# First norm's squares by ScalarE alone; splits, banks and fills around the last RWKV pairs; compression groups with ScalarE's copy of transposed probabilities

## The reference

```python
h = rms_norm(x, norm_mix_pre[l])
z = h @ w_in[l]
z_rwkv, z_nsa, z_gate = jnp.split(z, [RWKV_COLS, RWKV_COLS + NSA_COLS], axis=-1)
o_a = rwkv7_time_mix(z_rwkv, ...)       # 16 heads of 64, a scan over the tokens
o_b = nsa_attention(z_nsa, ...)         # 16 query heads in 4 groups
g_a, g_b = jnp.split(jax.nn.sigmoid(z_gate), 2, axis=-1)
m = g_a * (o_a @ w_branch_rwkv[l]) + g_b * (o_b @ w_branch_nsa[l])
x = x + rms_norm(m @ w_out[l], norm_mix_post[l])
```

## Time and profile before

| what | value |
|---|---|
| median of three runs | 1313.42 us (1313.29 to 1313.56) |
| the profiled execution, its own time | 1315.69 us |
| its span on the chip | 1313.8 us |
| TensorE busy | 1264.5 us, 96% |
| VectorE, ScalarE, GpSimd busy | 68%, 51%, 19% |
| mean granted clock of TensorE | 0.994 of full speed |
| read and written by DMA | 145 GB/s in the mean |

### The profile page before, as it was taken

One profiled execution on the slowest core, in us unless ns is written; L12 is line 12 of the kernel. 1 busy time (PEld: TensorE's weight loads), 2 busy tenths in 40 slices (PEclk: granted clock), 3 DMA queues, 4 the chain that ended last, 5 costly groups with the idle time before them and its releaser, 6 DMA issues.

```text
span 1313.8 us, 26575 instructions
## 1 busy us (share of the span) xinstructions
PE 1264.5 (96%) x10005; PEld 1133.7 (86%) x10005; DVE 899.3 (68%) x1764; ACT 667.1 (51%) x1276; POOL 247.6 (19%) x378
## 2 busy tenths in 40 slices
PE   7999999989889999999999999999999999999997
PEld 6989999888889988999988987888888977888886
DVE  7778888647745486787846566777745765877744
ACT  5465565443256645766535456534434576544332
POOL 1012222221455411233402000111200000122200
PEclk9999999999999999999999999999999999999999
DMA  8321122024311244445555422455554632455552
GB/s 330 126 98 66 66 79 86 34 84 164 139 64 65 72 175 172 173 179 192 189 192 200 177 84 77 162 191 192 184 194 166 196 126 97 161 180 179 185 193 94
DMA packets 27059, 189.95 MB, mean 145 GB/s; under 512 B 2992, under 2 KB 3248, under 8 KB 4816
## 3 DMA queue, kind: packets, MB, share of 16 engines
q1 hardware_dynamic: 25920, 182.61, 38.6%
q0 software_dynamic: 1040, 5.96, 1.4%
HBM read 186.47 MB, written 1.05 MB: 143 GB/s over the span
## 4 chain that ended last, share of the span: by engine, by line
PE 83%; DVE 7%; ACT 5%; DVEq 2%; issue 1%; DMA 1%; POOLq 1%; POOL 0%; ACTq 0%; SPq 0%
PE ps L612 33%; PE ps L560 13%; PE ps L673 12%; PE ps L675 6%; PE ps L927 3%; DVE ring_r L2071 1%; PE ps L585 1%; PE ps L766 1%; DVE w_lo L2084 1%; PE ps L592 1%; PE ps L944 1%; PE ps L584 1%; PE ps L827 1%; PE ps L1018 1%; PE ps L752 1%
## 5 line engine op out<-in xcount | busy, mean ns | idle before, releaser
L1528 ACT ACTIVATE w_hi<-ring 128x1024 fp32r<-128x1024 f32 x125 | 132.6, 1061 | 294.4 <-PE ps L612 155.3
L2084 DVE TENSOR_TENSOR w_lo<-ring,w_hi 128x1024 fp32r<-128x1024 f32 x125 | 155.4, 1243 | 127.9 <-ACT w_hi L1528 127.7
L673 PE MATMUL ps<-h_both,w_hi 128*128 128x512 f32 x672 | 237.7, 399 | 0.0
L675 PE MATMUL ps<-h_both,w_lo 128*128 128x256 f32 x672 | 188.7, 281 | 0.0
L612 PE MATMUL ps<-h_both,w_hi 128*128 128x256 f32 x912 | 165.7, 284 | 0.8 <-DVE w_lo L2090 0.8
L2090 DVE TENSOR_TENSOR w_lo<-ring,w_hi 128x1024 fp32r<-128x1024 f32 x125 | 157.4, 1259 | 0.0
L673 PEld LDWEIGHTS ps<-h_both,w_hi 128*128 128x128 f32 x672 | 126.3, 188 | 31.4
L560 PE MATMUL ps<-oT_r,ring_r 128*128 128x256 f32 x512 | 145.0, 283 | 0.0
L612 PEld LDWEIGHTS ps<-h_both,w_hi 128*128 128x128 f32 x912 | 142.5, 192 | 1.4 <-DVE w_lo L2090 1.2
L1533 ACT ACTIVATE w_hi<-ring 128x1024 fp32r<-128x1024 f32 x125 | 130.8, 1047 | 0.0
L612 PE MATMUL ps<-h_both,w_lo 128*128 128x256 f32 x456 | 129.0, 283 | 0.0
(11 more groups left out here) (446 smaller groups left out, 2959.8 us busy)
## 6 DMA issues: line engine op xcount, KB each, us to landing
ring<-in_weights SPq DMA_DIRECT2D x170, 1024.0 KB, 4.8
arena<-in_aux POOLq DMA_DIRECT2D x1, 2112.0 KB, 11.5
grow<-in_rows POOLq DMA_DIRECT2D x3, 512.0 KB, 4.7
cst<-in_consts SPq DMA_DIRECT2D x1, 1497.5 KB, 18.5
x<-in_x SPq DMA_DIRECT2D x2, 512.0 KB, 4.4
arena<-in_swbias POOLq DMA_DIRECT2D x1, 1024.0 KB, 10.3
arena<-arena POOLq DMA_DIRECT2D x1, 1024.0 KB, 8.8
out<-xn SPq DMA_DIRECT2D x4, 256.0 KB, 2.2
```

The lines of the kernel that those rows point to most:

```text
L673: pe.matmul(bank[:].rearrange("p (a t) -> p a t", a=2), hi, h_both[:, :, k, :], start=k == 0, stop=False)
L675: m = pe.matmul(bank[:, 0:S], lo, h_hi[:, k, :], start=False, stop=k == KT - 1)
L1528: act.activation(w_hi[:, half_of(u0, m), WH:], ring[:, (u0 + m) % RING, WH:], ACT.Copy).then_inc(w_hi_p, 1)
L2084: dve.tensor_tensor(w_lo[:, half_of(u0, m), WH:], ring[:, (u0 + m) % RING, WH:], w_hi[:, half_of(u0, m), WH:].bitcast(F32), ALU.subtract). ...
```

## The change

In the first norm ScalarE squares both halves and VectorE scales both; TensorE's transposes now wait for the identity and the small parameters, which raise one semaphore together. Around the last RWKV pairs, the two query pieces that stood in slots 3 and 5 of pair 6 go ahead of its phase; ScalarE's drain of query 0 goes ahead of its rows; the halves of the splits of units 18 to 20 are spread over other places; the four key and value units change banks (`ps[(m + 1) % 2]`), and three of VectorE's fills go behind its third drain. In the compression groups ScalarE copies the transposed probabilities, in place of VectorE; the products alternate between two banks; VectorE takes the second half of the subtraction for unit `ONE + 3` = 29, which GpSimd did whole; GpSimd stages the first two biases before that subtraction.

```diff
@@ line 382 @@
+def half_by_dve(m):
+    return m == ONE + 3
 def pool_units(m):
@@ line 456 @@
     sp.dma_start(x[:, 0, :], x_d[:, 0, :]).then_inc(x0_in, 16)
-    sp.dma_start(x[:, 1, :], x_d[:, 1, :]).then_inc(x1_ident_in, 16)
-    sp.dma_start(cst[:, 0:P], const_d[:, 0:P]).then_inc(x1_ident_in, 16)
+    sp.dma_start(x[:, 1, :], x_d[:, 1, :]).then_inc(x1_in, 16)
+    sp.dma_start(cst[:, 0:P], const_d[:, 0:P]).then_inc(params_in, 16)
     sp.dma_start(sml[:, n_gates:], small_d[:, n_gates:]).then_inc(params_in, 16)
@@ line 549 @@
             pe.wait_ge(one_lo_e, pool_units(m))
-        else:
-            pe.wait_ge(one_lo_d, m + 1 - pool_units(m))
+        if half_by_dve(m) or not by_pool(m):
+            pe.wait_ge(one_lo_d, m + 1 - pool_units(m) + sum(map(half_by_dve, range(m + 1))))
@@ line 808 @@
-    pe.wait_ge(x1_ident_in, 32)
+    pe.wait_ge(params_in, 32)
     for b in range(NB):
@@ line 1047 @@
         pieces = {PAIRS - 3: {1: 1, 2: 1, 5: 1, 9: 1, 11: 4},
-                  PAIRS - 2: {1: 1, 3: 1, 5: 2, 7: 1, 9: 1, 10: 1, 11: 1},
+                  PAIRS - 2: {1: 1, 5: 1, 7: 1, 9: 1, 10: 1, 11: 1},
                   PAIRS - 1: {1: 1, 2: 1, 3: 1, 4: 1, 5: 1, 6: 1, 7: 1, 8: 1, 10: 1, 11: 1}}.get(n)
+        if n == PAIRS - 2:
+            for _ in range(2):
+                next(fill, None)
         for slot in range(12):
@@ line 1115 @@
     g = (g_hi, g_lo)
-    pe.wait_ge(ev_lo, 4)
     for tile in range(2):
-        for _ in one_tile(ps[0][:, tile * S:(tile + 1) * S], 2 * PAIRS + 4, tile, g):
+        for _ in one_tile(ps[1][:, tile * S:(tile + 1) * S], 2 * PAIRS + 4, tile, g):
             pass
@@ line 1122 @@
     for m in range(5, 8):
+        pe.wait_ge(ev_lo, m - 1)
         if m >= 6:
-            pe.wait_ge(ev_lo, m - 1)
             pe.wait_ge(ev_hi, m - 5)
-        one_f_unit(ps[m % 2], 2 * PAIRS + m, g)
+        one_f_unit(ps[(m + 1) % 2], 2 * PAIRS + m, g)
@@ line 1184 @@
         for b in range(NB):
-            m = pe.matmul(ps[2][:, b * S:(b + 1) * S], cpT[:, b, :], Vblk[:, g, :], start=True, stop=True)
+            m = pe.matmul(ps[2 + g % 2][:, b * S:(b + 1) * S], cpT[:, b, :], Vblk[:, g, :], start=True, stop=True)
         m.then_inc(c_pv, 1)
@@ line 1618 @@
                    accum_out=stat[:, 0:1]).then_inc(sq_ready, 1)
-    act.wait_ge(first_sq, 3)
-    act.activation(xn[:, 1, :], x[:, 1, :], ACT.Copy, scale=stat[:, 5:6]).then_inc(first_xn, 1)
-    act.wait_ge(params_in, 16)
+    act.wait_ge(x1_in, 16)
+    act.activation(xn[:, 1, :], x[:, 1, :], ACT.Square, scale=1.0 / 32,
+                   accum_out=stat[:, 1:2]).then_inc(sq_ready, 1)
+    act.wait_ge(params_in, 32)
     for q in range(4):
@@ line 1734 @@
             take_query(1)
-        if powers:
-            rows(n + 1)
+            high_half(2 * PAIRS + 2, False)
         if n == PAIRS - 2:
             take_query(0)
+        if powers:
+            rows(n + 1)
         if front:
@@ line 1754 @@
             take_powers(n + 1, 1)
-        if past:
-            take_variance(n - 1)
         if n == PAIRS - 1:
             high_half(2 * PAIRS + 3, True)
+        if past:
+            take_variance(n - 1)
         if scan:
@@ line 1780 @@
             take_query(2)
-            split_one(2 * PAIRS + 4)
         if powers:
@@ line 1785 @@
             take_u(n, 3)
+        if n == PAIRS - 1:
+            split_one(2 * PAIRS + 4)
         if n == PAIRS - 2:
-            split_one(2 * PAIRS + 2)
+            high_half(2 * PAIRS + 2, True)
@@ line 1810 @@
         act.wait_ge(unit_done, U["nsa_q"] + m + 1)
-        src = ps[m % 2][0:HD, :].rearrange("p (a t) -> p a t", a=2)
+        src = ps[(m + 1) % 2][0:HD, :].rearrange("p (a t) -> p a t", a=2)
         if m < 6:
@@ line 1829 @@
         act.wait_ge(c_arg, g + 1)
-        if g:
-            act.wait_ge(c_pT, g)
         act.activation(cp_[:, :, 0:N_CMP], cs[:], ACT.Exp).then_inc(c_exp, 1)
+        act.wait_ge(c_tr, g + 1)
+        act.activation(cpT.rearrange("p b t -> p (b t)"), ps[1][:, 0:S], ACT.Copy).then_inc(c_pT, 1)
         if g == 0:
             take_mixer(0)
-    take_mixer(1)
-    split_one(ONE + 3)
+        if g == 2:
+            take_mixer(1)
+            split_one(ONE + 3)
     phase_end(act)
@@ line 2204 @@
         dve.memset(Zw[d][:, NC, :], 0.0)
-    dve.wait_ge(x1_ident_in, 32)
-    dve.tensor_tensor_reduce(out=xn[:, 1, :], in0=x[:, 1, :], in1=x[:, 1, :], scale=1.0 / D, scalar=0.0,
-                             op0=ALU.mult, op1=ALU.add, accum_out=stat[:, 1:2]).then_inc(first_sq, 1)
+    dve.wait_ge(x0_in, 16)
     dve.wait_ge(root_ready, 1)
     dve.tensor_scalar(xn[:, 0, :], x[:, 0, :], stat[:, 4:5], None, ALU.mult).then_inc(xn_ready, 1)
-    dve.wait_ge(params_in, 16)
+    dve.wait_ge(x1_in, 16)
+    dve.wait_ge(first_sq, 2)
+    dve.tensor_scalar(xn[:, 1, :], x[:, 1, :], stat[:, 5:6], None, ALU.mult).then_inc(first_xn, 1)
+    dve.wait_ge(params_in, 32)
     for q in range(4):
@@ line 2373 @@
             take_r(n, 0)
+        if n == PAIRS - 1:
+            low_half(2 * PAIRS + 2, False)
         dve.drain()
@@ line 2393 @@
             add_z(n + 1, 2)
+        if n == PAIRS - 1:
+            low_half(2 * PAIRS + 3, True)
         if scan:
             take_state(n, 1)
-        if n == PAIRS - 1:
-            split_one(2 * PAIRS + 3)
         next(steps, None)
@@ line 2400 @@
             take_r(n, 2)
+        if n == PAIRS - 1:
+            low_half(2 * PAIRS + 3, False)
         next(steps, None)
@@ line 2423 @@
         if n == PAIRS - 2:
-            split_one(2 * PAIRS + 2)
+            low_half(2 * PAIRS + 2, True)
@@ line 2440 @@
-    dve.memset(Vblk, 0.0)
-    dve.memset(cp_, 0.0)
-    dve.memset(kcmp, 0.0)
     for m in range(4, 8):
-        dve.wait_ge(unit_done, U["nsa_q"] + m + 1)
-        src = ps[m % 2][HD:P, :].rearrange("p (a t) -> p a t", a=2)
         if m == 5:
@@ line 2450 @@
             dve.drain()
+        dve.wait_ge(unit_done, U["nsa_q"] + m + 1)
+        src = ps[(m + 1) % 2][HD:P, :].rearrange("p (a t) -> p a t", a=2)
         if m < 6:
@@ line 2458 @@
             split_one(2 * PAIRS + 2 + m)
+        if m == 6:
+            dve.memset(Vblk, 0.0)
+            dve.memset(cp_, 0.0)
+            dve.memset(kcmp, 0.0)
@@ line 2519 @@
         dve.wait_ge(c_exp, g + 1)
-        if g + 1 < GROUPS:
-            cmp_args(g + 1)
         dve.tensor_reduce(cst8[:, 1, :], cp_[:, :, 0:N_CMP], AX, ALU.add)
         dve.drain()
+        if g + 1 < GROUPS:
+            cmp_args(g + 1)
         dve.tensor_scalar(cst8[:, 1, :], cst8[:, 1, :], 1e-30, None, ALU.max)
@@ line 2530 @@
                           cst8[:, 2, :].rearrange("p (b h) -> p b h", b=NB), gate, ALU.mult)
-        dve.wait_ge(c_tr, g + 1)
-        dve.tensor_copy(cpT.rearrange("p b t -> p (b t)"), ps[1][:, 0:S]).then_inc(c_pT, 1)
+        if g == 3:
+            low_half(ONE + 3, False)
         dve.wait_ge(c_pv, g + 1)
@@ line 2537 @@
                 o_rows[:, b, g * S:(g + 1) * S].rearrange("p (h d) -> p h d", d=HD),
-                ps[2][:, b * S:(b + 1) * S].rearrange("p (h d) -> p h d", d=HD),
+                ps[2 + g % 2][:, b * S:(b + 1) * S].rearrange("p (h d) -> p h d", d=HD),
                 cst8[:, 3, b * HPG:(b + 1) * HPG].unsqueeze(2).broadcast_to((P, HPG, HD)), ALU.mult)
@@ line 2833 @@
                                     one_hi(m)[:, part].bitcast(F32), ALU.subtract)
-        if not first:
+        if first == half_by_dve(m):
             lo.then_inc(one_lo_e, 1)
@@ line 2839 @@
         low_half(m, True)
-        low_half(m, False)
+        if not half_by_dve(m):
+            low_half(m, False)
+    def stage_bias(h):
+        pool.sem_inc(apart, 1)
+        pool.tensor_tensor(b_st[:, h % 2, :], dist, const("slope")[:, h:h + 1].broadcast_to((P, KEYS)),
+                           ALU.mult).then_inc(b_staged, 1)
@@ line 2844 @@
     pool.wait_ge(first_sq, 1)
-    for b, (squares, count, rooted) in enumerate(((sq_ready, 1, root_ready), (first_sq, 2, first_sq))):
+    for b, (squares, count, rooted) in enumerate(((sq_ready, 1, root_ready), (sq_ready, 2, first_sq))):
         pool.sem_inc(apart, 1)
@@ line 2919 @@
     split_one(ONE + 2)
+    for h in range(2):
+        stage_bias(h)
     split_one(ONE + 3)
@@ line 2927 @@
     for h in range(H):
-        pool.wait_ge(max_ready, NSA0 + 2 * h - 2)
-        pool.sem_inc(apart, 1)
-        pool.tensor_tensor(b_st[:, h % 2, :], dist, const("slope")[:, h:h + 1].broadcast_to((P, KEYS)),
-                           ALU.mult).then_inc(b_staged, 1)
+        if h >= 2:
+            pool.wait_ge(max_ready, NSA0 + 2 * h - 2)
+            stage_bias(h)
         for n, first in due.get(h, ()):
```

More of the change, by code:

```diff
@@ L2519, in _ @@
                 dve.wait_ge(c_exp, g + 1)
+                dve.tensor_reduce(cst8[:, 1, :], cp_[:, :, 0:N_CMP], AX, ALU.add)
+                dve.drain()
                 if g + 1 < GROUPS:
                     cmp_args(g + 1)
-                dve.tensor_reduce(cst8[:, 1, :], cp_[:, :, 0:N_CMP], AX, ALU.add)
```

(1 more changed line is left out.)

11 lines of the change are left out of this document (5 added, 6 removed).

## The result

The changed kernel takes **1301.5 us** (median of four executions, 1300.93 to 1302.33), the kernel before, run beside it, 1313.49 us. The ratio is 0.9907, with a 95% interval from 0.9895 to 0.9919: 12.0 us faster, where 15.2 us were forecast. That is inside the stated range of 1294.5 to 1303 us, and outside the 1296.5 to 1299.8 us that the forecast had without its rivals. The profiled execution is the shortest of the four, 1300.93 us with a span of 1298.3 us; of before it was longer than the median, 1315.69 us with a span of 1313.8 us.

A forecast was written before the change was run, and what follows sets the result against it. TensorE, busy 1264.5 of 1313.8 us, was taken as the bound, leaving its waits and half-clock time to gain. Norm -1.3, pairs -6.7 and compression -7.2 gave -15.2 us off the 1313.42 us median: 1298.2 us, range 1294.5 to 1303.

The forecast's parts named there:

- nothing there hangs on a fixed time, so the shift stays: Behind the changed places TensorE is bound by its own products, so the whole gain of 15.2 us reaches the end.
- (a): Before pair 6's phase: two query pieces, 1.43 us, fill TensorE's 1.34 us wait for ScalarE's rows; -1.4 us.
- (b): Start of pair 7's phase: 1.3 us new wait for unit 18's second half, less 0.8 us shorter old waits; +0.5 us.
- (c): Pair 7: the 2.29 us wait behind VectorE's subtractions for unit 19 goes, -2.3 us, and the low clock behind it, -1.7 us.
- (d): First key unit: in the other bank it no longer waits 0.69 us for ScalarE's drain of query 3; -0.7 us.
- (e): Key and value units: the 0.73 us wait goes and 1.0 us of the 1.39 us wait stands; -1.1 us.
- TensorE then waits for VectorE's last two multiplies (0.76 us) alone; I let 0.5 us stand: End of the compression: TensorE's 2.06 us wait for GpSimd's subtraction shrinks to 0.5 us; -1.5 us.
- the last -1.7 us: Behind the wait at the compression's end: the stretch at low clock goes with that wait; -1.7 us.
- The low clock comes back: Rival: new waits in (b) and the compression lower the clock, 1.7 us each; 1299.9 or 1301.6 us, chance 0.22.
- The norm's rival: First norm: GpSimd's power stays slow and only 0.3 us come; 1299.2 us, chance 0.10.
- slower than before: Rival: the clock stays low through the rebuilt stretch, 250 to 370 us; half of it gives 1328 us, chance 0.03.
- ScalarE becomes what the groups wait for: Compression: a 2.58 us ScalarE block delays the second group's exponential and the last wait passes 2 us; 1301.4 us, chance 0.10.

The follow-up runs named there:

- the run with two inputs: The changed kernel plus one VectorE product of x's second half with itself beside GpSimd's first power, its result unused; 1302.17 us in a single execution.
- the run with one input: The changed kernel plus two VectorE multiplications of x's second half by a constant in the first norm, results unused; 1301.98 us in a single execution.
- the pairs alone: The kernel before with only the change around the last RWKV pairs and the key and value units; 1307.97 us, ratio 0.9952.
- the run with the longer wait: The changed kernel with VectorE's result rows multiplied by one before the compression's phase end, so TensorE waits longer; median 1304.9 us.
- the compression alone: The kernel before with only the change to the compression, unit 29 and the biases; 1310.33 us, ratio 0.9965.

## Why the prediction was right, and where it was off

**The norm** was right to the tenth at the first weight product: -1.30 us, by the mechanism named. How much of it arrives further on is not shown. The first 32 weight products are the same in every kernel, but not equally long. Here they are in the traces of before, of the changed kernel and of the run with two inputs:

```profile
13.02 8.26 PE L827 MATMUL ps<-hT,ring 128*128 128x256 f32 x32
```

```profile
11.72 7.74 PE L831 MATMUL ps<-hT,ring 128*128 128x256 f32 x32
```

```profile
12.79 7.14 PE L831 MATMUL ps<-hT,ring 128*128 128x256 f32 x32 [0.26 <-DVE hT L2229]
```

Over the fourteen traces they take 7.14 to 8.42 us; from the product behind them to the end of the powers for pair 6 every trace takes 227.2 to 227.4 us. So of the -1.8 us in the table 1.3 us stand at the first weight product and 0.5 us come from these 32, which the prediction left out. In the trace of before they start 0.43 us apart up to 15.3 us and 0.22 us apart from there, as if at the two levels of the clock; the rows of granted clock read 1.00 there, so that cause is not shown. The eight traces of kernels whose lists are alike up to pair 6 reach the end of its powers at 246.26 to 247.42 us, the three with the old norm at 247.62 to 248.38. But the run with two inputs, whose first weight product comes 1.1 us later than the changed kernel's, reaches it at 246.94 us, and the one with one input, 0.8 us later, at 246.76 us. For this term the step "nothing there hangs on a fixed time, so the shift stays" is therefore open.

**The pairs** were right in sum and in each term: measured by further shifts. At the third chunk of pair 6 the shift is 3.2 us (261.65 to 258.45), so (a) is -1.4 us behind the 1.8 of the table (forecast -1.4). At the second chunk of pair 7 it is 2.7 (272.73 to 270.00), so (b) is +0.5 (forecast +0.5, with a wait of 1.06 us where 1.3 were taken). At the centring of the last pair it is 7.1 (288.65 to 281.52), so (c) with its clock is -4.4 (forecast -4.0). At line 893, now 897, ahead of the key units' products, it is 7.6 (296.20 to 288.59), so (d) is -0.5 (forecast -0.7), and to the 9.0 at the first scores (e) is -1.4 (forecast -1.1). In the median, the pairs alone gave -6.3 against -6.7. The wait of 2.28 or 2.29 us that (c) removed was followed by the low clock in each of the three traces that have it, so there the clock was rightly counted.

**The compression** had the two errors. The four waits went as forecast and the new wait for the exponential came, 1.20 us for the 1.4 taken. But the step "TensorE then waits for VectorE's last two multiplies (0.76 us) alone; I let 0.5 us stand" failed. The half of the subtraction that VectorE took over stands in VectorE's own list ahead of these multiplies, 1.22 us, so that the phase's end waited 2.04 us for VectorE where it had waited 2.06 us for GpSimd: 0 in place of -1.5. The run that moved this one instruction gave 1.17 us back. Against it stands a small surplus: from each group's transposes to its product TensorE took 3.60, 2.85, 3.14 and 3.13 us, and now takes 1.68, 1.67, 1.66 and 1.70, together 6.0 us less where 5.4 were forecast.

**The median** is where the rest went. The step "I subtract the sum from the median" failed: the sum was made from a trace of 1315.69 us, while the executions that make the median took 1313.29 to 1313.56 us. That trace has three low stretches: the two of the earlier trace rows, and one in a place that the change leaves alone, which the prediction did not name:

```profile
790.00:796.00 6.00, 6.00 (x27) 5.10 (x25) 3.42 (x12) 3.94 (x12) 0.00 (x0) 0.72 0.01 3
```

The terms of 1.7 us for the clock are true of the trace, not of each execution. Beside the run with the longer wait, the nine executions of the kernel before fall into two groups, six from 1313.32 to 1313.92 us and three from 1315.22 to 1315.44, about one such stretch apart. Across this study's traces, the wait of 2.0 to 2.1 us at the end of the compression was followed by half clock in 3 of 10 (before, the compression alone, and the run with two inputs). A price of 1.7 us on it is worth some 0.5 us in the mean, an estimate from these ten. So in the medians little of the last -1.7 us was there to be had, and as the wait itself stayed, the compression's part gained neither there. That is argued from times and shares: the executions of the median have no trace. In the spans of the traces the whole change is -15.5 us (forecast -15.2), in medians -12.0. The execution traced before took 2.2 us more than its median and that of the changed kernel 0.6 us less than its own, which makes most of this gap. The closeness of the traces is in part luck, too: 0.5 us of it come from the first weight products.

**The rivals.** "The low clock comes back" is true in part: one trace with the wait of 1.06 us in pair 7, that of the run with one input, has half clock behind it, the others do not; in the changed kernel's own trace there is none from 250 to 380 us. The norm's rival and "slower than before" fell. "ScalarE becomes what the groups wait for" did not come: the second group has no wait, and the last one's 1.20 us is less than the 1.4 us of the forecast itself. The measured 1301.5 us lies where the first two rivals put it (1299.9 or 1301.6, and 1301.4 us), by other causes: the overlooked subtraction, and terms from a long execution taken off the median. The stated range holds it because it was drawn around those rivals; that part is luck.

## What to carry to other kernels

Where a step is moved to another engine's list, read what stands behind it in that list and who waits for that; half a subtraction moved to the idle engine only handed the same wait from GpSimd to VectorE. Make the sum against several executions, not one trace: a stretch at half clock behind a wait of some 2 us is there in some executions and missing in others, so it counts by its share. A forecast of many small terms can be checked by the shift of the same instruction at a few places, which told here at once which part gave less. A gain ahead of a stretch whose own time varies between traces, as that of the first weight products does, is not yet a gain behind it.

## What the hardware showed

The low clock is no fixed follower of a wait's length. The wait of 2.0 us near 771 to 789 us (line 752, now 756), which no kernel here touched, was followed by half clock in 10 of 14 traces; the one of 2.0 to 2.1 us at the end of the compression in 3 of 10; one of 3.43 us in its only trace. Waits of 1.77 and 1.06 us were each followed by it once and in other traces not, and near 1020 to 1040 us it came in 5 of 14 traces, and in all five the waits there are no longer than 0.6 us. Each such stretch reads 0.72 over 6 us, so 1.7 us. What decides in a single execution stays open; no run here tells. The Trainium skill ("TensorE: Matmul & The Clock Gate", Part 1) says of a kernel's first products that how many of them run slowly varies from run to run of the same kernel. The three traces of the changed kernel agree: their first 32 weight products took 7.74, 8.20 and 7.62 us.

GpSimd's small instructions, too, can cost many times their length: 0.22 us became 1.23 us beside a VectorE product of 1.22 us, and 0.76 us beside scalings with one input. The prediction gave two inputs as the rule, though its sum let GpSimd's second root outlast VectorE's scaling "as it does now".
